# Opening modulation as one-column products on TensorE, output in eight transfers, carried sums in the attention

## What is computed

```python
mod = silu(c) @ ada_w[i] + ada_b[i]           # c: (1, 1024), ada_w[i]: (1024, 6144)
sh1, sc1, gt1, sh2, sc2, gt2 = split(mod, 6)
h = rmsnorm(x, norm_g[i, 0]) * (1 + sc1) + sh1
b_gate, c_gate, hv = split(h @ conv_w_in, 3)  # the opening product, 1024 x 3072
# ... stick-breaking attention, for each head, s < t:
ls_neg = log_sigmoid(-z)                      # z = q.k / sqrt(128)
log_rest = cumsum(log_fail, reverse=True) - log_fail
log_a = z + ls_neg + log_rest                 # A = exp(log_a), o = A @ v
```

## Time and profile before

| | us |
|---|---|
| median of 3 runs | 3007.37 |
| lowest, highest | 3000.99, 3010.88 |
| profiled execution, its own time | 2998.74 |
| its span | 2997.0 |
| TensorE busy in the span | 2860.0 (95%) |
| VectorE, ScalarE, GpSimd busy | 1596.3, 1052.8, 190.3 |
| mean granted TensorE clock | 0.985 |

### The profile page before, as it was taken

One profiled execution on the slowest core, in us unless ns is written; L12 is line 12 of the kernel. 1 busy time (PEld: TensorE's weight loads), 2 busy tenths in 40 slices (PEclk: granted clock), 3 DMA queues, 4 the chain that ended last, 5 costly groups with the idle time before them and its releaser, 6 DMA issues.

```text
span 2997.0 us, 47541 instructions
## 1 busy us (share of the span) xinstructions
PE 2860.0 (95%) x21352; PEld 2311.9 (77%) x21352; DVE 1596.3 (53%) x2264; ACT 1052.8 (35%) x1352; POOL 190.3 (6%) x151
## 2 busy tenths in 40 slices
PE   5999999899999989999999999899999998999999
PEld 4878888678888877888766767688888786788887
DVE  8766554463677654333366666554344657554342
ACT  3225233353233235234343232242123447532221
POOL 2010000201322110000100000010000000000000
PEclk9999999999999999999999999899999999999999
DMA  6644554120000032222220101032322220222321
GB/s 266 219 177 176 201 185 178 65 99 29 17 3 3 17 113 85 99 90 94 80 71 29 57 29 44 15 104 82 118 90 86 97 73 0 85 98 78 113 81 67
DMA packets 40379, 270.68 MB, mean 90 GB/s; under 512 B 4464, under 2 KB 4720, under 8 KB 12144
## 3 DMA queue, kind: packets, MB, share of 16 engines
q1 hardware_dynamic: 39744, 266.11, 25.3%
q10 hardware_dynamic: 432, 1.54, 0.1%
HBM read 265.54 MB, written 2.10 MB: 89 GB/s over the span
## 4 chain that ended last, share of the span: by engine, by line
PE 86%; DVE 8%; ACT 4%; issue 1%; DMA 0%; POOL 0%; SPq 0%; DVEq 0%; ACTq 0%
PE ps L648 21%; PE ps L649 21%; PE ps L654 21%; PE ps L2111 6%; PE ps L2887 1%; PE ps L1676 1%; PE ps L1659 1%; PE ps L1670 1%; PE ps L2795 1%; PE ps L2217 1%; DVE WL L405 1%; PE ps L2274 1%; PE ps L2268 1%; PE ps L2243 1%; PE ps L2235 1%
## 5 line engine op out<-in xcount | busy, mean ns | idle before, releaser
L648 PE MATMUL ps<-HH,WH 128*128 128x512 f32 x1928 | 767.0, 398 | 36.8 <-ACT HH L625 19.7
L649 PE MATMUL ps<-HH,WL 128*128 128x512 f32 x1928 | 756.5, 392 | 0.0
L654 PE MATMUL ps<-HL,WH 128*128 128x512 f32 x1928 | 731.7, 392 | 3.6 <-DVE HL L848 2.4
L405 DVE TENSOR_TENSOR WL<-ST,WH 128x2048 fp32r<-128x2048 f32 (+3 forms) x230 | 465.6, 2025 | 234.3 <-ACT WH L397 234.3
L397 ACT ACTIVATE WH<-ST 128x2048 fp32r<-128x2048 f32 (+1 forms) x211 | 383.4, 1817 | 311.5 <-PE ps L654 281.6
L648 PEld LDWEIGHTS ps<-HH,WH 128*128 128x128 f32 x1928 | 366.0, 190 | 125.1 <-issue 27.6
L654 PEld LDWEIGHTS ps<-HL,WH 128*128 128x128 f32 x1928 | 364.7, 189 | 83.9 <-DVE HL L600 4.1
L649 PEld LDWEIGHTS ps<-HH,WL 128*128 128x128 f32 x1928 | 366.3, 190 | 79.1 <-issue 3.8
L648 PE MATMUL ps<-GH,WH 128*128 128x512 f32 x928 | 361.0, 389 | 0.0
L649 PE MATMUL ps<-GH,WL 128*128 128x512 f32 x928 | 361.0, 389 | 0.0
L654 PE MATMUL ps<-GL,WH 128*128 128x512 f32 x928 | 359.7, 389 | 0.0
(11 more groups left out here) (381 smaller groups left out, 3511.1 us busy)
## 6 DMA issues: line engine op xcount, KB each, us to landing
ST<-w_m SPq DMA_DIRECT2D x64, 1024.0 KB, 4.9
ST<-w_gu SPq DMA_DIRECT2D x44, 1024.0 KB, 4.8
ST<-w_ada SPq DMA_DIRECT2D x40, 1024.0 KB, 6.3
ST<-w_dn SPq DMA_DIRECT2D x32, 704.0 KB, 4.0
ST<-w_gin SPq DMA_DIRECT2D x16, 1024.0 KB, 4.8
ST<-w_cin SPq DMA_DIRECT2D x12, 1024.0 KB, 4.9
ST<-w_rkv SPq DMA_DIRECT2D x12, 1024.0 KB, 4.9
W<-w_ada SPq DMA_DIRECT2D x16, 512.0 KB, 16.0
```

Source lines behind the costliest of these rows:

```text
L405: o = e.tensor_tensor(WL[:, j % 3, cut], ST[:, pos % 3, cut], WH[:, j % 3, cut].bitcast(F32), ALU.subtract)
L648: e.matmul(ps[:, :], wh[:, k, cs], H[:, k, :], start=(k == 0), stop=False)
L649: e.matmul(ps[:, :], wl[:, k, cs], H[:, k, :], start=False, stop=False)
L654: o = e.matmul(ps[:, :], wh[:, k, cs], L[:, k, :], start=False, stop=(k == kt - 1))
```

## The change

It does four things. (1) The 16 opening columns are computed by TensorE: `ada_w` is laid out with the contraction on partitions for these, and per k `tensor_shift` makes 2 x 8 float32 products, 128x128 stationary and one column of silu(c) moving, into one PSUM tile; ScalarE adds bias and forms the gain in three one-column activations. (2) GpSimd's multiplication by RST and VectorE's two operations are replaced by one scalar_tensor_tensor per k (as elsewhere in the kernel), and HL adds the shift itself. CROW is loaded behind the third chunk, its silu moved behind ScalarE's chunk 2. (3) In the attention GpSimd adds the log-fail columns of block j + 1 onto those of block j, for j = 2 and 1, once "rest" of j is done, so that each "rest" needs at most two products. (4) The result leaves in eight transfers of 256 KB, each behind its own residual.

```diff
-            d = f // KT % 2 if f < 2 * KT else f % 2
+            d = f % 2
...
+        def tensor_shift(e, k):
+            e.wait_ge(s_ad[k], 32)
+            e.wait_ge(*sml.free(("shift", k)))
+            for d in (1, 0):
+                for q in range(KT):
+                    o = e.matmul(sml.tile(("shift", k))[:, d:d + 1], W0[:, KT * d + k, P * q:P * q + P],
+                                 CSIL[:, q:q + 1], start=(q == 0), stop=(q == KT - 1))
+            o.then_inc(*norm_mm.up("shift", k))
...
+            e.wait_ge(*norm_act.at("silu columns"))
+            tensor_shift(e, 0)
             high, low = split_high("conv"), split_low("conv")
             for n, ks in ((0, range(3)), (1, range(3)), (0, (3,)), (1, (3,)), (0, (4,)), (1, (4,)), (0, (5,)),
                           (1, (5,)), (0, (6,)), (1, (6,)), (0, (7,)), (1, (7,))):
-                e.wait_ge(*lo.at(J["conv_in"][n]))
                 for k in ks:
+                    if n == 0 and k + 1 < KT:
+                        tensor_shift(e, k + 1)
+                    e.wait_ge(*lo.at(J["conv_in"][n]))
                     tensor_group(e, "conv_in", n, [2 * n, 2 * n + 1], k, HH, HL, high, low)
...
-            e.wait_ge(s_row, 16)
-            e.activation(CROW[:, :], CROW[:, :], ACT.Silu).then_inc(*norm_act.up("silu"))
+            e.wait_ge(s_cols, 16)
+            c0 = COLS["c"][0]
+            e.activation(CSIL, CC[:, c0:c0 + KT], ACT.Silu).then_inc(*norm_act.up("silu columns"))
             scalar_rms(e, "conv")
             scalar_high(e, 0)
             for k in range(KT):
-                e.wait_ge(*scan_pool.at("xr", k))
-                e.wait_ge(*norm_vec.at("conv", "gain", k))
-                e.activation(HH[:, k, :], HX[:, k, :], ACT.Identity, scale=SM[:, 8 + k:9 + k],
+                g = col("norm_g", k)
+                e.wait_ge(*norm_mm.at("shift", k))
+                e.activation(MOD[:, 8 + k:9 + k], sml.tile(("shift", k))[:, 1:2], ACT.Identity,
+                             bias=col("ada_b", KT + k)).then_inc(*norm_act.up("scale", k))
+                e.wait_ge(*norm_act.at("scale", k))
+                e.activation(SM[:, 8 + k:9 + k], MOD[:, 8 + k:9 + k], ACT.Identity, scale=g,
+                             bias=g).then_inc(*norm_act.up("gain", k))
+                e.activation(MOD[:, k:k + 1], sml.tile(("shift", k))[:, 0:1], ACT.Identity,
+                             bias=col("ada_b", k)).then_inc(*norm_act.up("shift", k))
+                e.wait_ge(*norm_act.at("shift", k))
+                e.wait_ge(*norm_vec.at("conv", "t", k))
+                e.activation(HH[:, k, :], tmp.tile(("split", "conv", k)), ACT.Identity,
                              bias=modcol(0, 0, k)).then_inc(*half.up("conv", k))
                 if k == 2:
                     scalar_high(e, 1)
             scalar_high(e, 2)
+            e.wait_ge(s_row, 16)
+            e.activation(CROW[:, :], CROW[:, :], ACT.Silu).then_inc(*norm_act.up("silu"))
...
             for k in range(KT):
                 e.wait_ge(*tmp.free(("split", "conv", k)))
+                e.wait_ge(*norm_act.at("gain", k))
+                e.scalar_tensor_tensor(out=tmp.tile(("split", "conv", k)), in0=X[:, k, :], scalar=SM[:, 8 + k:9 + k],
+                                       in1=RST[:, :], op0=ALU.mult,
+                                       op1=ALU.mult).then_inc(*norm_vec.up("conv", "t", k))
+                if k == 0:
+                    vector_low(e, 0)
+                else:
+                    vector_first_low(e, k - 1)
+                if k == 3:
                     vector_low(e, 1)
+            vector_first_low(e, KT - 1)
             vector_low(e, 2)
...
-                    for j2 in range(j, 4):
-                        w2 = T - P * j2
-                        o = e.matmul(pr[:, w_ - w2:w_], tb("tri" if j2 == j else "ones"),
-                                     LFT[h % 4][:, OFF[j2]:OFF[j2] + w2], start=(j2 == j), stop=(j2 == 3))
+                    o = e.matmul(pr[:, 0:w_], tb("tri"), LFT[h % 4][:, OFF[j]:OFF[j] + w_], start=True, stop=(j == 3))
+                    if j < 3:
+                        if j < 2:
+                            e.wait_ge(*att_pool.at("carried", h, j + 1))
+                        o = e.matmul(pr[:, P:w_], tb("ones"), LFT[h % 4][:, OFF[j + 1]:OFF[j + 1] + w_ - P],
+                                     start=False, stop=True)
...
+        def pool_attend(e):
+            for h, j in ATTEND:
+                if 0 < j < 3:
+                    w_ = T - P * j
+                    L = LFT[h % 4]
+                    e.wait_ge(*att_mm.at("rest", h, j))
+                    if j == 1:
+                        e.wait_ge(*att_pool.at("carried", h, 2))
+                    e.tensor_tensor(L[:, OFF[j] + P:OFF[j] + w_], L[:, OFF[j] + P:OFF[j] + w_],
+                                    L[:, OFF[j + 1]:OFF[j + 1] + w_ - P], ALU.add).then_inc(*att_pool.up("carried", h, j))
...
-            e.dma_start(CROW[:, :], crow).then_inc(s_row, 16)
             e.dma_start(CC[:, :], cols).then_inc(s_cols, 16)
             for pos, ks in ((0, (0,)), (1, (1, 2)), (2, (3, 4, 5, 6, 7))):
                 for k in ks:
                     load_first(e, k)
                 sync_load(e, pos)
+            e.dma_start(CROW[:, :], crow).then_inc(s_row, 16)
...
-            e.wait_ge(*res.at("dn11", 7))
-            e.dma_start(out, X[:, :, :]).then_inc(s_out, 16)
-            e.wait_ge(s_out, 16)
+            for m in range(KT):
+                e.wait_ge(*res.at("dn11", m))
+                e.dma_start(out[:, m, :], X[:, m, :]).then_inc(s_out, 16)
+            e.wait_ge(s_out, 16 * KT)
```

More of the change, by code:

```diff
@@ L267, in build @@
         HX = place("HX", [P, KT, T], F32, hh_at + 16384)
+        CSIL = EX[:, 0:KT]
         U = place("U", [P, 2, T + 2], F32, ar_at + 32768 + 16384)
@@ L317, in build @@
         sumsq, scan_pool, gdn_pool = tally("squares_added"), tally("scan_pool"), tally("gdn_pool")
+        att_pool = tally("att_pool")
         sched = order()
@@ L454, in vector_sums @@
         def vector_sums(e, pos, n):
+            e.wait_ge(*norm_act.at("silu"))
+            e.wait_ge(s_cols, 16)
             tile = ST[:, pos % 3, :].rearrange("p (f a b) -> p f a b", f=2, a=2)
@@ L457, in vector_sums @@
             for q in range(2):
-                modulation(e, 2 * n + q, tile[:, q], 2 * n + q - 2 if n > KT else (KT - 1, 2 * KT - 1)[q])
+                modulation(e, 2 * n + q, tile[:, q], 2 * n + q - 2 if n > KT else None)
         def vector_gain(e, tag, g0, layer, which, s):
@@ L746, in plan_conv @@
             plan_rms("conv")
+            for k in range(KT):
+                sml.use(("shift", k), norm_act, "shift", k)
             plan_split("conv")
@@ L807, in scalar_conv, with vector_first_low @@
                         e.wait_ge(*out_vec.at("y", m))
-                        e.wait_ge(*ada.at(KT - 1))
+                        e.wait_ge(*norm_mm.at("shift", KT - 1))
                         e.activation(GH[:, k, :], CV[:, m % 2, :], ACT.Identity).then_inc(*out_act.up("conv_hi", k))
             scalar_residual(e, "conv_out", "mlp0")
[L813 to L823, removed]
+        def vector_first_low(e, k):
+            e.wait_ge(*half.at("conv", k))
+            e.wait_ge(*norm_act.at("shift", k))
+            e.scalar_tensor_tensor(out=HL[:, k, :], in0=tmp.tile(("split", "conv", k)), scalar=modcol(0, 0, k),
+                                   in1=HH[:, k, :].bitcast(F32), op0=ALU.add,
+                                   op1=ALU.subtract).then_inc(*norm_vec.up("conv", "lo", k))
         def vector_conv(e):
@@ L830, in vector_conv @@
                 e.tensor_tensor(ACC[:, :], ACC[:, :], HX[:, k, :], ALU.add).then_inc(*norm_vec.up("conv", "sum", k))
-            vector_first(e, 0, KT)
-            vector_first(e, 0, 0)
-            vector_first_gain(e, 0)
             vector_rms(e, "conv")
-            vector_first(e, 1, KT + 1)
-            vector_low(e, 0)
+            e.wait_ge(*norm_vec.at("conv", "rstd"))
             for k in range(KT):
-                t = tmp.tile(("split", "conv", k))
                 e.wait_ge(*tmp.free(("split", "conv", k)))
[L840 to L853, removed]
+                e.wait_ge(*norm_act.at("gain", k))
[7 more added lines that the diff above has]
+                if k == 3:
                     vector_low(e, 1)
+            vector_first_low(e, KT - 1)
             vector_low(e, 2)
@@ L2936, in vector_sb @@
             vector_residual(e, "so", None, 0, 0, "ffn1")
+        def pool_attend(e):
[8 more added lines that the diff above has]
+                                    L[:, OFF[j + 1]:OFF[j + 1] + w_ - P], ALU.add).then_inc(*att_pool.up("carried", h, j))
         def pool_sb(e):
+            pool_attend(e)
             pool_squares(e, "ffn1")
@@ L3076, in layout @@
     packed = np.concatenate([cols[n] for n in COLS], axis=1).astype(np.float32, copy=False)
```

(3 more changed lines are left out.)

## The result

The changed kernel takes **3027.85 us** (median of four runs, 3024.78 to 3030.42) against 3005.80 (four runs, 3000.99 to 3010.88): a ratio of 1.0079, 95% interval 1.006 to 1.0098, slower by 0.8%. The prediction was 3038 with a range of 3012 to 3054. The profiled execution after took 3027.69 us, span 3025.9; before 2998.74, span 2997.0. Between the two profiled executions the difference is 28.95 us, where the working of the prediction had 30.7.

What follows compares the result with a forecast made beforehand. TensorE, with 86% of the last-ending chain, was taken as the bound. Opening +39, attention -4.5 and end -3.8 made +30.7 us: 3029.4 from the profiled 2998.7, 3038 on the median of 3007.4; range 3012 to 3054.

Steps and rivals of the forecast that it cites:

- The price of a product: Opening: a one-column float32 product costs 0.23 us, a burst of 16 takes 3.6 at full clock and 6.9 low.
- Rival D: Opening: weight loads hide better in runs of 16; at half the price -12 us, 2995; chance 4%.
- C: Opening: a weight load costs the same at either clock, low burst 3.5 us; +11 us in all, 3018; chance 5%.
- The clock: Opening: TensorE's clock is low in one-column bursts, 1.2 GHz, and comes up only in the dense stretches between.
- Rival A: Opening: bursts count as activity and run at 2.4 GHz; opening +14 us, +6 in all, 3013; chance 15%.
- Rival B: Opening: a 3.6 us burst does not bring down a clock already raised; +19 us in all, 3026; chance 15%.
- The sum of the opening: Opening: bursts, dense groups and waits put chunk 2's start at 102.8 against 63.6, +39 us, bounds +27 to +51.
- Attention, -4.5: Attention: shorter "rest" products save TensorE 6.9 us over 8 heads, of which -4.5 us was counted.
- two thirds arrive: Attention: ScalarE, busy 33.33 of 37.70 us, lets only two thirds of TensorE's 6.9 us saving through.
- The fear that GpSimd holds VectorE: Attention: GpSimd's 16 adds might hold VectorE some 9 us in all, against 11 us idle in each half.
- End, -3.8: End: the last 256 KB lands in 2.5 us where 2 MB took 6.3, so -3.8 us.
- The last step, +8.7: Whole kernel: the profile of before lay 8.7 us under its median; adding this to 3029.4 gave 3038.

Runs made afterwards that it cites:

- Experiment 1: The changed kernel with the moving operand of each burst product widened to the same silu column repeated 128 times: 3006.40 us, one run.
- experiment 2: The kernel before with only the attention's carried sums and the output in eight transfers, opening as before: 2993.59 us against 3003.27, ratio 0.997.
- experiment 5: The kernel before with carried sums and eight transfers, the sixteen additions on VectorE instead of GpSimd: 2994.69 us, one run.
- Experiment 6: The kernel before, unchanged, profiled once more: 3005.41 us, where its first profile took 2998.74.

## Why the prediction was right, and where it was not

**Where the change acts.** Right: nothing behind chunk 2 absorbed the delay, and its start could be carried through to the end: +39.2 at chunk 2 and +40.9 at 1500 us.

**The price of a product.** Right. 0.23 us each at full clock from two rows gave 3.6 a burst, measured 3.63 as a record and 3.49 from start to start; 6.9 at low clock from the earlier trace rows, measured 6.82 and 6.69. (The factor 1.96 on 3.6 gives 7.1, not the 6.9 that was written.) Rival D fell with it, and so did C: a low burst takes 1.88 times a high one. The Trainium skill ("TensorE: Matmul & The Clock Gate", LDWEIGHTS), which gives a load at one price, 107 ns (32 of them are 3.4 us, an estimate; the prediction wrote 3.5), does not hold for these bursts.

**The clock.** Right, and from two short stretches. Experiment 1 shows the cause, which the prediction had only argued. Rival A, the rule of the same page that TensorE is to be kept busy (Why this matters for your kernels), is contradicted by the windows from 68 to 76: 8.00 us busy of 8.00, clock 0.50. Rival B said that a burst does not bring the clock down once it is up; the clock fell behind the burst at 58.46. B's number, 3026, is closer to the median than mine, but by a start of chunk 2 at 91 and an offset that wasn't there.

**The sum of the opening.** 102.8 predicted, 102.79 measured; that it is this close is luck, since errors cancel. For k = 4 to 7 I had bursts of 5.3, 21.2 in all, and the four take 18.4 (3.63, 6.82, 4.15, 3.84); for the two dense groups behind each I had 4.6, and behind the bursts at 58.46, 67.95, 80.26 and 90.16 they take 5.6 to 6.0. Together the four rounds take 41.4 (58.46 to 99.87) where I had 39.6; the last two groups give it back, 2.9 for 4, and the start of the four, 58.46 for 59.2. Three of the four bursts begin high and run at or near the full price (3.63, 4.15, 3.84), the second is low throughout (6.82), and it is mostly the dense products behind a burst that pay for the fall. The waits were 0.3 to 0.4 for one k at low clock (0.5 predicted), 0.99 once at high (1.3), and 0.98 for chunk 1's split (1.4). The predicted waits rest on 2.2 us for two activations, two VectorE operations and hand-overs, where 0.40 + 1.38 + 0.25 is 2.0.

**Attention, -4.5.** Right in sign and undersized: -6.1, and -6.8 in experiment 2. "rest" for j = 0 takes 1.50 from start to start (2606.10 to 2607.60), as predicted, and 2.16 before. The term that was mis-sized is "two thirds arrive": nearly all of it did, 6.1 us of the 6.2 by which TensorE's busy time fell. I read ScalarE's 33.33 of 37.70 us as a limit. The groups shown above say that its waits were for VectorE, which waited for "rest": a loop through three engines in which the shortened product was the late one. The fear that GpSimd holds VectorE came true at half the size, 32 masks of each kind longer by 0.07 us on average, 4.5 us in all where I had some 9, and cost nothing (experiment 5).

**End, -3.8.** -4.3: 256 KB land in 2.1 us, not the 2.5 of a load.

**The last step, +8.7, is the one that was wrong.** Up to there the sum stood at 3029.4; the profiled execution took 3027.69 and the median 3027.85. I carried the distance between the profiled execution of before and its median over to the changed kernel. Experiment 6 shows what the distance is: another execution of the same kernel takes 3005.41, 6.7 more than the first, and 7.3 more in the delta rule by the clock there. Part of it was also the small sample: the median of three was 3007.37, and before ran 9 and 11 times beside the experiments with medians of 3003.17 to 3003.63. The profile of after has the short form (398.3) and sits on its own median all the same, so nothing was to be added. Its four executions lie between 3024.78 and 3030.42, while those of before reach from 2997.47 to 3010.88; why none of after's lies as far above its profile is open. The medians differ by 22.1 us, the profiled executions by 28.95, and the forecast, 30.7 above the median that it started from, is 9 too high against the medians for that reason.

## What to carry to other kernels

Before work is put on TensorE, count the columns that it streams, not the time that it keeps the engine busy: here products with one column cost as much as products with 128 (3.63 and 3.73 us a burst) and took the clock away from the dense products around them. Widening the moving operand gave 21 us back; giving TensorE such work mainly in the gap in which it idles gave a start of chunk 2 earlier than before's (56.46 for 63.60). Before the distance between a profiled execution and a median is added to a forecast, ask in which stretch it lies: one whose length changes between executions of the same kernel says nothing of the change.

## What the runs showed of the hardware

- Sixteen float32 products with a 128x128 stationary operand take 3.63 us with one column and 3.73 with 128 at 2.4 GHz. In the window from 68 to 72, within a one-column burst, the loads of the stationary operand are recorded busy 4.00 of 4.00 us: that they, and not the columns, set the price up to that width is the reading that fits both.
- VectorE's masks, operations on two SBUF operands, are held up by a GpSimd add that runs at the same time. On average they go from 292 to 365 ns and from 283 to 351, but the time lies in single ones, here the second row beside the first, and the third with GpSimd idle:

```profile
2565.16 0.87 POOL L2962 TENSOR_TENSOR LF<-LF 128x256 f32<-128x256 f32 x1 [1.63 <-PE ps L2811]
2565.36 0.82 DVE L2855 TENSOR_TENSOR ZS<-ZS,TB 128x128 f32<-128x128 f32 x1
...
2573.19 0.28 DVE L2855 TENSOR_TENSOR ZS<-ZS,TB 128x128 f32<-128x128 f32 x1
```

The Trainium skill ("SBUF — State Buffer", SBUF: two separate sides) has the two engines lock a pair of ports against each other in just that case, a VectorE operation with two SBUF inputs against a GpSimd operation that reads SBUF, so that the one that comes second waits; the trace agrees, 0.82 us for 0.28. VectorE's subtraction that reads PSUM keeps its 686 to 691 ns, which shows nothing here: none of those wide ones ran beside an add.
- The same code takes 398.2 to 407.3 us in one stretch, by how often the clock falls in it: 6.8 to 17.2 us of loss by the granted clock.
